# Attention probabilities turned in 32x32 blocks by VectorE and carried across partitions by GpSimd and ScalarE, in place of TensorE transposes, for 12 of 18 jobs

## The chip, the cores and the metric

The kernel runs on one core of a Trainium2 chip. The metric is device time in microseconds: 2020.84 us, median of 3 runs (2015.42 to 2021.22). TensorE (PE) multiplies matrices and writes to PSUM, VectorE (DVE), ScalarE (ACT) and GpSimd (POOL) work elementwise, and the SP, ACT and POOL queues issue DMAs.

## The reference, cut to what matters

A decoder layer for a prompt of 2048 tokens and 8 sequences of 8 sample tokens. One input projection feeds three groups; their outputs (width 2048) go through one output projection. The change lies in the third group, attention of 4 heads of 128 into 256 memory tokens:

```
qx = q_x.reshape(B, T, XA_HEADS, XA_HEAD_DIM)
s = jnp.einsum('bthd,bshd->bhts', qx, mem_k).astype(jnp.float32) * (XA_HEAD_DIM ** -0.5)
p = jax.nn.softmax(s, axis=-1).astype(x.dtype)
y_xa = jnp.einsum('bhts,bshd->bthd', p, mem_v).reshape(B, T, XA_WIDTH) * jax.nn.silu(z_x)
...
y = jnp.concatenate([y_ml, y_cv, y_xa], axis=-1) @ w_out
```

The scores come out with tokens on partitions, and the product with the values needs the 256 memory tokens there: every 128x128 piece of the probabilities must be transposed.

## The kernel before

Three stages follow each other: `project` (to about 1346 us), `attend` (to about 1606 us) and `recur`. The engines' programs are written out by hand, each engine runs its own in order, and they wait on counting semaphores. The change is in `attend`.

`attend` runs a loop over 16 tiles of 128 prompt tokens (t = 0 to 15) and a last one, t = 16, for the samples. I number loops by t. Its work comes as 18 jobs: 16 prompt tiles and two sample jobs, which stand ahead of the prompt tiles 7 and 11. Loop t handles the jobs that `due(t)` gives, normally the one of tile t + 1. In a normal loop TensorE does:

- `out_conv(t)`: 24 matmuls of the output projection over the convolution's half. Every fp32 product is made of three (high by high, high by low, low by high). The first waits until `add(t - 1)` has added the previous tile out of the same PSUM bank.
- `turn_p(n)`: 8 transposes of the probabilities (4 heads, 2 halves of 128 memory tokens) into two PSUM banks.
- `scores(n + 1)`: 4 matmuls for the next job.
- `out_xa(t)`: 24 matmuls over the attention's half.
- `weigh_values(n)`: 16 matmuls of the values by `pT`, the turned probabilities.

VectorE does `gate` (the product with the gate path out of PSUM), `xa_low` (low half of the gated tile), `wm_low` (two weight halves, loops 11 to 14), `turn_keys` (one block transpose of 128x1024 of the sample keys, loops 2 to 9), `conv_low`, `largest` (maxima), `normalise`, and `add` of the tile. ScalarE does `xa_high`, `wm_high`, `load_keys` (it issues four DMAs for one sample sequence's keys, loops 0 to 7), `conv_high`, `p_back` (two copies from PSUM to `pT`) and `exps` (four exponentials). GpSimd issues one value load for each of the first eight loops. SP loads tiles and weights and stores the sums in a scratch tensor.

The sample keys are loaded in 32x32 blocks into the tile `ksq`, which lies in the buffer `raw` and has four slots, and VectorE's transpose turns every block where it stands. At t = 14 SP loads the q and k of the first two tiles of `recur` into the same buffer.

## Time and profile before

| | |
|---|---|
| median of 3 runs | 2020.84 us |
| the profiled execution, its time | 2021.7 us |
| its span | 2019.8 us |
| TensorE busy | 2008.2 us, 99% |
| VectorE, ScalarE, GpSimd busy | 1474.5, 912.9, 874.6 us |
| granted TensorE clock, mean | 0.999 of full speed |

The span is what the profile covers, the time of the execution lies 1.9 us above it. All times in rows are from the start of the span. An engine's idle time costs only where TensorE comes to wait for it.

### The profile page before, as it was taken

To read this page: it belongs to the slowest core of one execution; us is meant where nothing else is said; L and a number is where in the kernel's file an instruction comes from. 1 tells how busy PE (TensorE), PEld (TensorE's weight loads), DVE (VectorE), ACT (ScalarE), POOL (GpSimd) and SP (SyncE) were. 2 spreads that over 40 slices of the span, in tenths; PEclk is the share of its full clock that TensorE was granted. 3 is DMA by queue.
4 is the path that set the end of the run, shared out by engine and by line. 5 is a ranking of instruction groups with operands and counts; after the bars stand their busy time and mean duration, and the time that the engine had idled before them with its cause. 6 is when DMAs were issued, how large, how long until landed. Compare 5 with 4: busy or idle time off the path is not lost.

```text
span 2019.8 us, 34158 instructions
## 1 busy us (share of the span) xinstructions
PE 2008.2 (99%) x12151; PEld 1877.8 (93%) x12151; DVE 1474.5 (73%) x2336; ACT 912.9 (45%) x1863; POOL 874.6 (43%) x721
## 2 busy tenths in 40 slices
PE   9999999999999999999999999999999999999998
PEld 6999999999999999999999999998888888888886
DVE  7777787798778877897778767654445468777775
ACT  5554445445444455454454455442324333433332
POOL 2556555585555565575555555520000122222220
PEclk9999999999999999999999999999999999999999
DMA  6655667555646676555445566578746788888765
GB/s 205 155 142 142 150 152 162 128 141 124 152 122 152 158 171 134 137 143 122 120 131 138 126 157 144 134 212 188 172 115 183 201 250 261 272 239 237 235 180 121
DMA packets 600151, 333.69 MB, mean 165 GB/s; under 512 B 331296, under 2 KB 563888, under 8 KB 599984
## 3 DMA queue, kind: packets, MB, share of 16 engines
q1 hardware_dynamic: 561824, 312.90, 59.5%
q10 hardware_dynamic: 37008, 14.43, 2.9%
q0 software_dynamic: 1152, 4.19, 0.6%
q8 instruction: 98, 1.61, 0.4%
q14 instruction: 69, 0.57, 0.1%
HBM read 237.87 MB, written 93.58 MB: 164 GB/s over the span
## 4 chain that ended last, share of the span: by engine, by line
PE 93%; DVE 2%; SPq 2%; DMA 1%; issue 1%; ACT 0%; POOL 0%; DVEq 0%; POOLq 0%; ACTq 0%
PE bank L742 21%; PE bank L744 21%; PE bank L743 21%; PE bank L2294 3%; PE bank L2296 2%; PE bank L2295 2%; PE bank L2264 2%; PE bank L2249 2%; PE bank L1650 1%; PE bank L1651 1%; PE bank L1652 1%; PE bank L1636 1%; PE bank L1639 1%; PE bank L1637 1%; PE bank L1601 1%; PE bank L1566 1%
## 5 line engine op out<-in xcount | busy, mean ns | idle before, releaser
L742 PE MATMUL bank<-xh,wh 128*128 128x352 f32 x2688 | 869.3, 323 | 0.9 <-DVE stage L1111 0.9
L744 PE MATMUL bank<-xh,wl 128*128 128x352 f32 x2688 | 867.0, 323 | 0.0
L743 PE MATMUL bank<-xl,wh 128*128 128x352 f32 x2688 | 863.6, 321 | 0.0
L1093 DVE TENSOR_TENSOR wl<-raw,wh 128x512 fp32r<-128x512 f32 x384 | 407.4, 1063 | 166.5 <-ACT wh L881 165.5
L742 PEld LDWEIGHTS bank<-xh,wh 128*128 128x128 f32 x2688 | 504.6, 188 | 3.8 <-issue 2.0
L743 PEld LDWEIGHTS bank<-xl,wh 128*128 128x128 f32 x2688 | 507.4, 189 | 0.3 <-issue 0.2
L744 PEld LDWEIGHTS bank<-xh,wl 128*128 128x128 f32 x2688 | 506.3, 188 | 0.0
L903 ACT ACTIVATE snap<-bank 128x352 f32<-128x352 f32 x384 | 178.5, 465 | 374.3 <-PE bank L744 374.2
L881 ACT ACTIVATE wh<-raw 128x512 fp32r<-128x512 f32 x384 | 240.6, 628 | 156.8 <-PE bank L744 155.6
L1093 DVE TENSOR_TENSOR wl<-wt,wh 128x512 fp32r<-128x512 f32 x288 | 246.8, 860 | 85.1 <-ACT wh L881 84.2
L692 POOL TENSOR_TENSOR stage<-snap 128x352 f32<-128x352 f32 x96 | 100.8, 1050 | 440.7 <-ACT snap L903 428.1
L881 ACT ACTIVATE wh<-wt 128x512 fp32r<-128x512 f32 x288 | 180.2, 626 | 118.9 <-PE bank L744 112.7
L676 POOL TENSOR_TENSOR wt<-raw 128x512 f32<-128x512 f32 x96 | 153.6, 1600 | 56.0 <-DMA raw<-in_w_in 42.1
L683 POOL TENSOR_TENSOR wt<-raw,wt 128x512 f32<-128x512 f32 x96 | 154.8, 1613 | 49.8 <-DVE wl L1093 49.8
L1111 DVE TENSOR_TENSOR stage<-bank,snap 128x352 f32<-128x352 f32 x288 | 149.0, 517 | 34.8 <-PE bank L744 30.6
L2143 POOL TENSOR_TENSOR work<-area,mask 128x512 f32<-128x512 f32 x16 | 20.7, 1295 | 336.8 <-DMA area<-scr_a 211.2
L679 POOL TENSOR_TENSOR wt<-raw,wt 128x512 f32<-128x512 f32 x96 | 156.0, 1625 | 8.1 <-DVE wl L1093 0.7
L680 POOL TENSOR_TENSOR raw<-raw 128x512 f32<-128x512 f32 x96 | 158.7, 1653 | 0.0
L2294 PE MATMUL bank<-wm_h,out_yh 128*128 128x512 f32 x240 | 117.1, 488 | 0.0
L2296 PE MATMUL bank<-wm_h,out_yl 128*128 128x512 f32 x240 | 94.3, 393 | 0.0
L2295 PE MATMUL bank<-wm_l,out_yh 128*128 128x512 f32 x240 | 94.0, 392 | 0.0
L2725 DVE SCALAR_TENSOR_TENSOR m_wide<-m_wide,wcb,bank 128x257 f32<-128x257 f32 x120 | 56.9, 475 | 49.6 <-PE bank L2264 48.4
(346 smaller groups left out, 2599.0 us busy)
## 6 DMA issues: line engine op xcount, KB each, us to landing
raw<-in_w_in SPq DMA_DIRECT2D x72, 1024.0 KB, 5.8
raw<-in_w_in SPq DMA_DIRECT2D x48, 512.0 KB, 5.6
scr_vob<-stage SPq DMA_DIRECT2D x192, 88.0 KB, 3.6
scr_qk<-stage SPq DMA_DIRECT2D x48, 352.0 KB, 5.2
raw<-scr_qk SPq DMA_DIRECT2D x16, 1024.0 KB, 8.8
area<-scr_vob SPq DMA_DIRECT2D x32, 512.0 KB, 8.0
scr_acc<-x_res SPq DMA_DIRECT2D x17, 512.0 KB, 6.2
m_acc<-scr_acc SPq DMA_DIRECT2D x17, 512.0 KB, 7.6
```

The source lines that it names most:

```text
L676: pool.tensor_tensor(wt[:, 0], b12, b11, ALU.subtract).then_inc(S["t_ready"], 1)
L679: pool.tensor_tensor(wt[:, 1], b22, wt[:, 0], ALU.subtract).then_inc(S["t_ready"], 1)
L680: pool.tensor_tensor(b12, b22, b12, ALU.subtract).then_inc(S["t_ready"], 1)
L683: pool.tensor_tensor(wt[:, 2], b21, wt[:, 1], ALU.subtract).then_inc(S["t_ready"], 1)
L742: pe.matmul(out, wh[:, b, k, :], xh[:, b, k, :], start=(first and k == 0), stop=False, skip_group_check=True)
L743: pe.matmul(out, wh[:, b, k, :], xl[:, b, k, :], start=False, stop=False, skip_group_check=True)
L744: m = pe.matmul(out, wl[:, b, k, :], xh[:, b, k, :], start=False, stop=(k == 3), skip_group_check=True)
L881: act.activation(halves(q, b)[0], source(q, b), ACT.Copy).then_inc(S["w_high"], 1)
L903: act.activation(snap[:, n, :], g if n == 1 else b, ACT.Copy).then_inc(S["snap"], 1)
L1093: dve.tensor_tensor(low, source(q, b), high.bitcast(F32), ALU.subtract).then_inc(S["w_low"], 1)
L1111: dve.tensor_tensor(out, src, snap[:, add, :], ALU.add).then_inc(S["out_dve"], 1)
L2294: pe.matmul(out, h[:, k, :], wmh[:, k, c], start=(k == 0), stop=False)
```

## The change

Jobs 0 and 1, the two sample jobs and the job right behind each keep the way over TensorE (`by_pe`, 6 jobs). The other 12 (`by_block`, handled in loops 1 to 5, 7 to 9 and 11 to 14) go as follows. VectorE turns every 32x32 block of the probabilities within itself with one transpose of 128x1024 into slot 3 of `ksq` (`turn_blocks`), behind `xa_low`. A block (g, f) of every 128x128 piece must then move from partition group g to group f. That takes 16 copies, each of 32 partitions by 8 runs of 32 elements, for all heads and halves at once: ten by GpSimd (`move_blocks`) and six by ScalarE (`p_moves`), the latter behind `load_keys` and ahead of `conv_high`. TensorE's `weigh_values` waits for all 16. `turn_p` and `p_back` are left out for these jobs. The keys keep three slots. SP's load of `q` and `k` for `recur` is split: the first half still at t = 14, the second at t = 15, behind the last copy. GpSimd's value loads move from a row of their own into the loop. In `project` two semaphores are merged with others, and in `recur` two waits name new counts.

```diff
+    psq = ksq[:, 3, :].rearrange("p (h s t) -> p h s t", h=H, s=2)
...
         jobs.append(("t", t))
     at = {job: n for n, job in enumerate(jobs)}
     s_at = [at["s", 0], at["s", 1]]
+
+    by_pe = [n for n, (kind, t) in enumerate(jobs) if n < 2 or "s" in (kind, jobs[n - 1][0])]
+    by_block = [n for n in range(len(jobs)) if n not in by_pe]
+    POOL_MOVES = [(g, f) for g in range(4) for f in range(4)][:10]
+    ACT_MOVES = [(g, f) for g in range(4) for f in range(4)][10:]
+
+    def turned_by_pe(n):
+        return sum(x < n for x in by_pe)
+
+    def turned_in_blocks(n):
+        return sum(x < n for x in by_block)
+
+    def p_block(tile, part, column):
+        return tile[SQ * part:SQ * (part + 1), :, :, SQ * column:SQ * (column + 1)]
 
     def due(t):
 
...
                 load_x(t + 1)
             if t == WM_FIRST + KM // 2:
                 sp.wait_ge(S["s_KT_ready"], DB)
-                for a in range(2):
-                    sp.dma_start(qk_tiles(raw)[:, a, :, :],
-                                 w["qk"][:, :, a * P:(a + 1) * P].rearrange("f p t -> p f t")).then_inc(S["qk_loaded"], 16)
+            if t >= NT - 2:
+                a = t - (NT - 2)
+                if a:
+                    sp.wait_ge(S["p_moved"], 16 * len(by_block))
+                sp.dma_start(qk_tiles(raw)[:, a, :, :],
+                             w["qk"][:, :, a * P:(a + 1) * P].rearrange("f p t -> p f t")).then_inc(S["qk_loaded"], 16)
 
     @block.gpsimd
     def _(pool):
...
         pool.affine_select(out=smask[:, :], in_=smask[:, :], compare_op=ALU.is_ge, fill=MASKED, base=0,
                            pattern=[[-32, 4], [0, DT]], channel_multiplier=1).then_inc(S["mask_ready"], 1)
         pool.wait_ge(S["mask_ready"], 3)
-        for b in range(DB):
+        def load_values(b):
+            if b >= DB:
+                return
             if b == 0:
                 pool.wait_ge(S["wx_low"], 4)
             else:
                 pool.wait_ge(S["xa_split"], b)
             pool.dma_start(V[:, b, :, :], mem_v[0, b].rearrange("(a s) h d -> s a (h d)", s=P)).then_inc(S[f"s_V_loaded{b // 4}"], 16)
+
+        def move_blocks(n):
+            if n in by_pe:
+                return
+            pool.wait_ge(S["p_squared"], turned_in_blocks(n) + 1)
+            wait(pool, S["pv_summed"], sum(k == "t" for k, _ in jobs[:n]))
+            wait(pool, S["s_pv_summed"], sum(k == "s" for k, _ in jobs[:n]))
+            for g, f in POOL_MOVES:
+                pool.tensor_copy(p_block(pT, f, g), p_block(psq, g, f)).then_inc(S["p_moved"], 1)
+
+        for t in range(NT):
+            load_values(t)
+            for n in due(t):
+                move_blocks(n)
 
     @block.tensor
     def _(pe):
...
                     m.then_inc(S["scores_summed"], 1)
 
         def turn_p(n):
+            if n in by_block:
+                return
             pe.wait_ge(S["p_ready"], 4 * n + 4)
-            wait(pe, S["pT_ready"], 2 * n)
+            wait(pe, S["pT_ready"], 2 * turned_by_pe(n))
             for g in range(4):
                 for s in range(2):
                     m = pe.transpose(bank[TURN[g // 2]][:, (g % 2) * NM + s * P:(g % 2) * NM + (s + 1) * P],
...
         def weigh_values(n):
 
             kind, t = jobs[n]
-            pe.wait_ge(S["pT_ready"], 2 * n + 2)
+            if n in by_pe:
+                pe.wait_ge(S["pT_ready"], 2 * turned_by_pe(n) + 2)
+            else:
+                pe.wait_ge(S["p_moved"], 16 * (turned_in_blocks(n) + 1))
             wait(pe, S["xa_gated"], sum(k == "t" for k, _ in jobs[:n]))
             wait(pe, S["s_pv_copied"], sum(k == "s" for k, _ in jobs[:n]))
             if kind == "t":
...
             if n >= len(jobs):
                 return
             act.wait_ge(S["nb_ready"], n + 1)
-            wait(act, S["p_turned"], 2 * n)
+            wait(act, S["p_turned"], 2 * turned_by_pe(n))
+            wait(act, S["p_squared"], turned_in_blocks(n))
             for g in range(4):
                 act.activation(pr[:, g, :], bank[SCORE[g // 2]][:, (g % 2) * NM:(g % 2 + 1) * NM], ACT.Exp,
                                bias=nb[:, g:g + 1], scale=XA_SCALE, accum_out=sums[:, g:g + 1]).then_inc(S["exp_ready"], 1)
+
+        def p_moves(n):
+            wait(act, S["pv_summed"], sum(k == "t" for k, _ in jobs[:n]))
+            wait(act, S["s_pv_summed"], sum(k == "s" for k, _ in jobs[:n]))
+            act.wait_ge(S["p_squared"], turned_in_blocks(n) + 1)
+            for g, f in ACT_MOVES:
+                act.activation(p_block(pT, f, g), p_block(psq, g, f), ACT.Copy).then_inc(S["p_moved"], 1)
 
         def p_back(n):
             wait(act, S["pv_summed"], sum(k == "t" for k, _ in jobs[:n]))
             wait(act, S["s_pv_summed"], sum(k == "s" for k, _ in jobs[:n]))
             for i in range(2):
-                act.wait_ge(S["p_turned"], 2 * n + i + 1)
+                act.wait_ge(S["p_turned"], 2 * turned_by_pe(n) + i + 1)
                 act.activation(pT[:, 2 * i:2 * i + 2, :, :],
                                bank[TURN[i]].ap().rearrange("p (h s t) -> p h s t", h=2, s=2), ACT.Copy).then_inc(S["pT_ready"], 1)
 
...
             if b >= DB:
                 return
             act.wait_ge(S["wx_low"], 4)
-            wait(act, S["s_KT_ready"], b - 3)
+            wait(act, S["s_KT_ready"], b - 2)
             for j in range(4):
-                act.dma_start(ksq[SQ * j:SQ * (j + 1), b % 4, :].rearrange("p (h i c) -> p h i c", h=H, c=SQ),
+                act.dma_start(ksq[SQ * j:SQ * (j + 1), b % 3, :].rearrange("p (h i c) -> p h i c", h=H, c=SQ),
                               mem_k[0, b, :, :, SQ * j:SQ * (j + 1)].rearrange("(i r) h c -> r h i c", r=SQ)
-                              ).then_inc(S[f"s_K_loaded{b % 4}"], 16)
+                              ).then_inc(S[f"s_K_loaded{b % 3}"], 16)
 
         def wm_high(k):
             if 0 <= k < KM:
...
                 wm_high(2 * (t - WM_FIRST - 1) + n)
             if t:
                 load_keys(t)
-            conv_high(t + 1)
             todo = due(t)
             for n in todo:
-                p_back(n)
+                if n in by_block:
+                    p_moves(n)
+            conv_high(t + 1)
+            for n in todo:
+                if n in by_pe:
+                    p_back(n)
                 if n == todo[-1]:
                     exps(n + 1)
                 else:
...
 
             if not 0 <= b < DB:
                 return
-            dve.wait_ge(S[f"s_K_loaded{b % 4}"], 64 * (b // 4 + 1))
-            dve.transpose(KT[:, b, :, :].rearrange("p h s -> p (h s)"), ksq[:, b % 4, :]).then_inc(S["s_KT_ready"], 1)
+            dve.wait_ge(S[f"s_K_loaded{b % 3}"], 64 * (b // 3 + 1))
+            dve.transpose(KT[:, b, :, :].rearrange("p h s -> p (h s)"), ksq[:, b % 3, :]).then_inc(S["s_KT_ready"], 1)
 
         def xa_low(t):
             dve.wait_ge(S["xa_high"], t + 1)
...
             ch.sync()
             for g in range(4):
                 dve.tensor_scalar(pr[:, g, :], pr[:, g, :], rsum[:, g:g + 1], None, ALU.mult).then_inc(S["p_ready"], 1)
+
+        def turn_blocks(n):
+            dve.wait_ge(S["p_ready"], 4 * n + 4)
+            wait(dve, S["p_moved"], 16 * turned_in_blocks(n))
+            dve.transpose(ksq[:, 3, :], area[:, 0:1024]).then_inc(S["p_squared"], 1)
 
         def gate(t):
             dve.wait_ge(S[f"xz_loaded{t % 2}"], 16 * (t // 2 + 1))
...
             else:
                 dve.wait_ge(S["cleared"], 1)
             xa_low(t)
+            for n in due(t):
+                if n in by_block:
+                    turn_blocks(n)
             for n in range(2):
                 wm_low(2 * (t - WM_FIRST - 1) + n)
             turn_keys(t - 2)
...
         pool.wait_ge(S["res_added"], 2)
         pool.wait_ge(S["wm_high"], 1)
         pool.wait_ge(S["acc_stored0"], 16)
-        for b in range(4):
-            pool.wait_ge(S[f"s_K_loaded{b}"], 64 * 2)
+        for b in range(3):
+            pool.wait_ge(S[f"s_K_loaded{b}"], 64 * (3 - b // 2))
         for a in range(2):
             pool.wait_ge(S[f"s_V_loaded{a}"], 16 * 4)
         cleared = S["cleared"]
```

On TensorE, in loop 2, the rows between `out_conv` (L1639, after the change L1678) and `out_xa` (L1650, L1689) are, before:

```order
L1639 MATMUL bank<-convw,out_yl 128x512
L1587 MATMUL bank<-ident,area 128x128 [waits pT_ready_attend,p_ready_attend]
L1587 MATMUL bank<-ident,area 128x128 x7
L1566 MATMUL bank<-work,area 128x256 [waits xq_loaded1_attend,exp_ready_attend]
L1566 MATMUL bank<-work,area 128x256 x3
L1650 MATMUL bank<-x_wx_h,out_yh 128x512 [waits xa_split_attend]
L1651 MATMUL bank<-x_wx_l,out_yh 128x512
```

and with the change:

```order
L1678 MATMUL bank<-convw,out_yl 128x512
L1600 MATMUL bank<-work,area 128x256 [waits xq_loaded1_attend,exp_ready_attend]
L1600 MATMUL bank<-work,area 128x256 x3
L1689 MATMUL bank<-x_wx_h,out_yh 128x512 [waits xa_split_attend]
L1690 MATMUL bank<-x_wx_l,out_yh 128x512
```

The transposes L1587 are gone and nothing stands in their place; `scores` follows the convolution at once.

On ScalarE, in loop 3, from `xa_high` (L1706, L1745) to `exps` (L1714, L1754), before:

```order
L1706 ACTIVATE out_yh<-area 128x512 [waits out_summed_attend,xa_gated_attend]
L1732 DMA raw<-in_cache_mem_k 32x32x32 [waits s_KT_ready_attend,wx_low_attend]
L1732 DMA raw<-in_cache_mem_k 32x32x32 x3
L1698 ACTIVATE out_yh<-area 128x512 [waits cv_used_attend,yc_loaded1_attend]
L1722 ACTIVATE area<-bank 128x512 [waits p_turned_attend,pv_summed_attend]
L1722 ACTIVATE area<-bank 128x512 [waits p_turned_attend]
L1714 ACTIVATE area,work<-bank,work 128x256 [waits p_turned_attend,nb_ready_attend]
L1714 ACTIVATE area,work<-bank,work 128x256 x3
```

and with the change:

```order
L1745 ACTIVATE out_yh<-area 128x512 [waits out_summed_attend,xa_gated_attend]
L1779 DMA raw<-in_cache_mem_k 32x32x32 [waits s_KT_ready_attend,wx_low_attend]
L1779 DMA raw<-in_cache_mem_k 32x32x32 x3
L1762 ACTIVATE area<-raw 32x8x32 [waits p_squared_attend,pv_summed_attend]
L1762 ACTIVATE area<-raw 32x8x32 x5
L1737 ACTIVATE out_yh<-work 128x512 [waits cv_used_attend,yc_loaded0_attend]
L1754 ACTIVATE area,work<-bank,work 128x256 [waits p_squared_attend,p_turned_attend,nb_ready_attend]
L1754 ACTIVATE area,work<-bank,work 128x256 x3
```

The six copies L1762 stand between the issue of the keys (L1732, L1779) and `conv_high` (L1698, L1737), and the two `p_back` copies L1722 are gone.

On SP's queue, from the store of tile 13 to the first gate loads of `recur` (L1401, L1402), before:

```order
L1502 DMA scr_acc<-x_res 128x1024 [waits res_added_attend]
L1498 DMA x_res<-in_x_prompt 128x1024 [waits acc_stored1_attend]
L1531 DMA raw<-scr_qk 128x16x128 [waits s_KT_ready_attend]
L1531 DMA raw<-scr_qk 128x16x128
L1502 DMA scr_acc<-x_res 128x1024 [waits res_added_attend]
L1498 DMA x_res<-in_x_sample 64x1024 [waits acc_stored0_attend]
L2020 UNCONDITIONAL_BRANCH
L1401 DMA area<-scr_negr 128x4x128 [waits cv_split_attend,xa_gated_attend,cleared_attend]
L1402 DMA area<-scr_a 128x4x128
```

and with the change:

```order
L1517 DMA scr_acc<-x_res 128x1024 [waits res_added_attend]
L1513 DMA x_res<-in_x_prompt 128x1024 [waits acc_stored1_attend]
L1549 DMA raw<-scr_qk 128x16x128 [waits s_KT_ready_attend]
L1517 DMA scr_acc<-x_res 128x1024 [waits res_added_attend]
L1513 DMA x_res<-in_x_sample 64x1024 [waits acc_stored0_attend]
L1549 DMA raw<-scr_qk 128x16x128 [waits p_moved_attend]
L2079 UNCONDITIONAL_BRANCH
L1401 DMA area<-scr_negr 128x4x128 [waits cv_split_attend,xa_gated_attend,cleared_attend]
L1402 DMA area<-scr_a 128x4x128
```

The second `raw<-scr_qk` has moved past a store and a load, to right ahead of the gate loads of `recur`.

## Rows read from the trace of the kernel before

**Rows 1.** The page, busy time of each engine, its share of the span and instructions
```profile
PE 2008.2 (99%) x12151; PEld 1877.8 (93%) x12151; DVE 1474.5 (73%) x2336; ACT 912.9 (45%) x1863; POOL 874.6 (43%) x721
```

**Rows 2.** Busy time in loops 3 and 7: length, then each engine
```profile
1396.77:1412.06 15.29, 15.29 (x81) 13.15 (x81) 7.39 (x14) 4.16 (x12) 0.72 (x1) 1.00 0.79 190
1463.40:1478.77 15.37, 15.37 (x82) 13.15 (x81) 8.33 (x19) 5.29 (x18) 0.00 (x0) 1.00 0.71 163
```

**Rows 3.** The chain that ended last, 1372 to 1560 us: start, us, what
```profile
1417.52 0.87 PE bank L1587 x8
...
1425.58 1.78 PE bank L1601 x16
...
1543.70 1.78 PE bank L1601 x16
```

**Rows 4.** Timeline of ScalarE, loops 2 and 3: start, us, instruction, idle before
```profile
1382.29 4.90 ACTq L1732 DMA_DIRECT2D raw<-in_cache_mem_k  x4
...
1397.59 4.62 ACTq L1732 DMA_DIRECT2D raw<-in_cache_mem_k  x4
1402.32 0.64 ACT L1698 ACTIVATE out_yh<-work 128x512 fp32r<-128x512 f32 x1 [4.11 <-PE bank L1639]
```

**Rows 5.** Timeline of VectorE, loop 3
```profile
1398.24 0.69 DVE L1811 TENSOR_TENSOR out_yl<-area,out_yh 128x512 fp32r<-128x512 f32 x1 [0.70 <-ACT out_yh L1706]
1398.85 1.24 DVE L1806 STREAM_TRANSPOSE s_kv<-raw 128x1024 f32<-128x1024 f32 x1
1402.99 0.69 DVE L1798 TENSOR_TENSOR out_yl<-work,out_yh 128x512 fp32r<-128x512 f32 x1 [2.89 <-ACT out_yh L1698]
```

**Rows 6.** Timeline of ScalarE, then VectorE, loop 7
```profile
1466.60 4.53 ACTq L1732 DMA_DIRECT2D raw<-in_cache_mem_k  x4
1471.23 0.63 ACT L1698 ACTIVATE out_yh<-work 128x512 fp32r<-128x512 f32 x1 [4.06 <-issue]
...
1477.26 1.28 DVE L1853 TENSOR_TENSOR x_res<-x_res,bank 128x512 f32<-128x512 f32 x2
```

**Rows 7.** Timeline: an add that TensorE waits for, and the matmuls behind
```profile
1412.13 0.40 PE L1637 MATMUL bank<-convw,out_yh 128*128 128x512 f32 x1
...
1600.59 0.69 DVE L1853 TENSOR_TENSOR x_res<-x_res,bank 128x512 f32<-128x512 f32 x1 [1.96 <-PE bank L1652]
...
1601.67 0.39 PE L1637 MATMUL bank<-convw,out_yh 128*128 128x512 f32 x1
```

**Rows 8.** Groups of ScalarE's instructions, 1345 to 1606 us
```profile
L1692 ACT ACTIVATE x_wx_h<-raw 128x1024 fp32r<-128x1024 f32 x4 | 4.0, 1056 | 2.0 <-PE bank L744 2.0
...
L1698 ACT ACTIVATE out_yh<-work 128x256 fp32r<-128x256 f32 x1 | 0.4, 418 | 4.1 <-PE bank L1639 4.1
```

**Rows 9.** Timeline of ScalarE, start of the stage
```profile
1345.79 2.97 ACT L1692 ACTIVATE x_wx_h<-raw 128x1024 fp32r<-128x1024 f32 x3 [1.96 <-PE bank L744]
```

**Rows 10.** Groups of GpSimd's instructions, whole span
```profile
L676 POOL TENSOR_TENSOR wt<-raw 128x512 f32<-128x512 f32 x96 | 153.6, 1600 | 56.0 <-DMA raw<-in_w_in 42.1 <-DVE wl L1093 13.8
...
L2147 POOL TENSOR_TENSOR m_wide<-raw,area 128x256 f32<-128x256 f32 x60 | 49.2, 830 | 16.3 <-PE bank L2250 16.3
...
L2165 POOL TENSOR_SCALAR m_few<-m_few 128x4 f32<-128x4 f32 x16 | 3.1, 193 | 66.1 <-ACT area L2474 41.8 <-ACT m_wide L2474 24.2
```

**Rows 11.** One line of VectorE in the first stage: ns min/median/max
```profile
L1093 DVE TENSOR_TENSOR wl<-raw,wh x384: 647/1012/3711, 36.7 to 1329.1; 128x512 fp32r<-128x512 f32 x192
```

**Rows 12.** Timeline of SP's queue, end of the stage
```profile
1578.67 3.06 SPq L1531 DMA_DIRECT2D raw<-scr_qk  x2
...
1596.76 1.64 SPq L1413 DMA_DIRECT2D area<-scr_z  x1
1601.31 3.60 SPq L2077 DMA_DIRECT2D scr_acc<-x_res  x1
```

**Rows 13.** Timeline of VectorE, loop 11
```profile
1542.71 0.68 DVE L1853 TENSOR_TENSOR x_res<-x_res,bank 128x512 f32<-128x512 f32 x1
```

More of the change, by code:

```diff
@@ L658, in _ @@
         pool.memset(eps[:, :], EPS).then_inc(S["eps_ready"], 1)
-        pool.memset(ident[:, :], 0.0).then_inc(S["ident_zero"], 1)
-        pool.wait_ge(S["ident_zero"], 1)
+        pool.memset(ident[:, :], 0.0).then_inc(S["ident_ready"], 1)
+        pool.wait_ge(S["ident_ready"], 1)
         pool.affine_select(out=ident[:, :], in_=ident[:, :], compare_op=ALU.not_equal, fill=1.0, base=0,
@@ L787, in turn_states @@
             pe.transpose(bank[7][0:72, 0:P], cnew.ap().rearrange("p s w j -> p (s w j)"), ident[:, :]).then_inc(S["states_turned"], 1)
-        pe.wait_ge(S["ident_ready"], 1)
+        pe.wait_ge(S["ident_ready"], 2)
         for k in range(WARM):
@@ L1324, in _ @@
         dve.wait_ge(S["gains_turned"], 1)
-        dve.tensor_copy(gcol[:, :], bank[7][:, 0:2 * KD]).then_inc(S["gains_ready"], 1)
-        dve.wait_ge(S["gains_ready"], 1)
+        ch.step(dve.tensor_copy(gcol[:, :], bank[7][:, 0:2 * KD]))
+        ch.sync()
         for u in range(2):
@@ L2208, in turn_keys @@
                 pe.wait_ge(before["exp_ready"], 4 * (NT + 2))
-                pe.wait_ge(before["pT_ready"], 2 * (NT + 2))
+                pe.wait_ge(before["pT_ready"], 2 * 6)
             wait(pe, S["t1_ready"], 4 * t)
```

## The prediction

> **What bounds the kernel now.** I read the page's busy times first: TensorE is busy 2008.2 of a span of 2019.8 us [rows 1]. So the only things worth looking for are work taken from TensorE and waits put in front of it. The change touches the middle stage (memory attention and the first half of the output projection, 1346 to 1606 us), so next I read busy time per loop: loop 3, from one end of the value matmuls to the next, is 15.29 us long and TensorE is busy in all of it, VectorE in 7.39, ScalarE in 4.16; loop 7 is 15.37 long and just as full, but VectorE and ScalarE have 8.33 and 5.29 [rows 2]. The chain that ended last runs along TensorE there: a loop holds one group of 8 transposes of 0.87 us and ends with the 16 value matmuls of 1.78 us [rows 3]. The timelines of ScalarE and VectorE then tell how far behind TensorE their chain runs [rows 4, 5, 6], and that decides this case.
>
> **Part 1, the transposes go: the gain.** In 12 loops TensorE no longer issues the 8 transposes. With no wait in their place a loop takes 15.30 - 0.87 = 14.43 us, and 12 x 0.87 = 10.4 us leave the path [rows 3]. The two ScalarE copies out of PSUM go too; they lay behind the wait for the maxima and freed nothing.
>
> **Part 2, VectorE turns blocks.** One transpose of 128x1024 stands behind the low half of the gated tile. The same operation on keys takes 1.24 us [rows 5]. In loop 3 the low half ends at 1398.93; the new transpose would end near 1400.2 and the key transpose near 1401.4, before VectorE's next input (the convolution's low half, 1402.99) is there. So it is covered by the idle time before 1402.99, in key loops and in the plain ones. In loops 11 to 14 two 128x1024 subtractions fill that time instead. In loop 11 the first add starts at 1542.71; pushed back by 1.24 and with 0.68 for itself it ends at 1544.63. TensorE goes on 0.39 after an add (1601.28 to 1601.67) [rows 7], at 1545.02. Unstalled, its second convolution matmul follows the end of the value matmuls by 0.07 (1412.06 to 1412.13), here 1543.70 + 1.78 + 0.07 - 0.87 = 1544.68 [rows 3, 7, 13]. Loss 0.3 us; uncovered fully it would be 1.24.
>
> **Part 3, six ScalarE copies ahead of the convolution's high half.** No copy of 32x8x32 is in the trace. The nearest is a 128x256 copy of 418 ns [rows 8]; three 128x1024 copies of 1056 ns took 2.97 us in a row, so (2.97 - 1.06) / 2 = 0.96 from start to start, 0.10 less than one lasts [rows 8, 9]. Lower value 0.32 each, 1.92 for six. Upper, if a change of partition group empties the engine, 0.42 each, 2.5 for six. I take 0.32, since all copies in this stage overlap so. What stands ahead of them in loops 1 to 5 and 7 is the issue of four key DMAs, which keeps the queue 4.62 to 4.90 us [rows 4]. In loop 3 it ends at 1402.21 and the high half starts at 1402.32; nothing is free there, and the whole 1.92 moves the high half. Behind it on the path: low half, maxima, exponentials, normalising, then the add of the output tile, for which TensorE's next convolution waits. Loop 7 shows this chain without a pause: high half at 1471.23, first add from 1477.26 for half of 1.28, so 6.7 us [rows 6].
> Loop 2: 1382.29 + 4.90 + 0.05 + 1.92 + 6.7 + 0.39 = 1396.25, against 1396.77 + 0.07 - 0.87 = 1395.97 unstalled: 0.3 us lost. Loop 3: 1397.59 + 4.62 + 9.06 = 1411.27 against 1411.26: nothing. VectorE's second add also ends some 0.2 us after the next gate could have begun, which makes the next loop late. I take 0.25 for each of loops 1 to 5, 1.3 us.
> Loop 7 comes after a sample job and begins late: its issue ends at 1466.60 + 4.53 = 1471.13, plus 9.06 is 1480.19, against 1478.77 + 0.07 - 0.87 = 1477.97. Loss 2.2 us [rows 2, 6].
> Loops 8 and 9 issue no keys: ScalarE waits there for TensorE anyway and the six copies are covered. In loops 12 to 14 they follow the weight halves and end about when the convolution releases the high half. With no cover each block would cost up to 1.9 to 2.5.
>
> **Part 4, ten GpSimd copies.** GpSimd had nothing but one value load a loop. They start when the blocks are turned (about 3.5 us into a loop) and must end by 14.43 - 1.78 = 12.65, when the value matmuls are due. Bounds: 0.19 us, the cost of a 4 element operation, and 0.83, a 128x256 product with two inputs; in the first stage 128x512 takes 1.60, half of which is 0.80 [rows 10]. One input and 256 elements lie between; I take 0.5, so ten end at 8.5, covered by 4 us.
> They share something with VectorE, though: the same subtraction of 128x512 takes 647 ns at best and 1012 as a median in the first stage, beside a busy GpSimd [rows 11], and 0.69 here [rows 5]. The convolution's low half now runs at about 8.4 us, under the last copies, and in loop 11 the two subtractions do. I put 0.15 on each of five key loops after the first (with loop 7) and 0.2 on loop 11: 1.0 us, bounds 0 and 0.4 on each of eleven.
> The Trainium skill (SBUF — State Buffer, Who interferes with whom) has a stricter rule: a VectorE instruction with two SBUF inputs and a GpSimd instruction that reads SBUF exclude each other for a whole instruction. By that rule a low half waits for at most one copy, so by it, with the 0.5 that I took, the sum would lose up to 0.5 a loop where I have 0.15, some 2 us more; no run yet shows how many hit.
>
> **Part 5, the queues.** The keys now have three slots; the wait asks for a transpose of the loop before, long done. The two halves of the first q and k tiles (two 1 MB DMAs, 3.06 us of issue at 1578.67) part: the second goes behind the last store of the stage and ahead of the next stage's gates. SP's queue is busy from there to 1596.76 + 1.64 = 1598.40 and idle until 1601.31, so 1.5 us more of issue fit into 2.9 [rows 12]. The next one took 3.60 us to issue, a sign of full rings, so I put 0.7 us on this place, bounds 0 and 4. What is behind it are the gates and value loads of the next stage's first tiles. Moving the count of a semaphore to another name, in the first stage, costs nothing.
>
> **Sum.** -10.4 + 0.3 (loop 11) + 1.3 + 2.2 (key loops) + 1.0 + 0.7 = -4.9 us. The profiled execution took 2021.7 us, 0.9 above the median of the runs, and would take 2016.8; against the median of 2020.84 this is **2015.9 us**.
>
> **Rivals.**
> All of it hidden. If the issue of keys ends earlier once the loops are arranged anew, or the high half's chain shortens by the 2 us that I charge, the loops are TensorE's at 14.43: 2020.84 - 10.4 = 2010.4. For it: six of the twelve loops issue no keys at all. Against: in loop 3 0.1 us was free. Chance 0.15.
> ScalarE's copies do not overlap. Then 0.6 more in loops 2 to 5, 7 and 11, 3.6 us, and with a low half that hits a GpSimd copy each time about 1 more: 2020.4, no change. Against: copies of this stage overlap. Chance 0.17.
> GpSimd's copies are late, the one on the slower side. Its place is the wait of the value matmuls. It decides from (12.65 - 3.5) / 10 = 0.91 us a copy on, and outweighs the 0.87 at 1.0. At 1.1 the matmuls wait for 3.5 + 11 - 12.65 = 1.9 us in each of the 12 loops, 1.0 more than is saved: 2020.84 + 12 = 2032.8. For it: strided runs of 32 elements between partition groups, of which no row speaks, and neighbours of 0.80 and 0.83. Against: these read twice. Chance 0.14.
> The forecast itself: 0.52; its own range is 2012.5 to 2018.
> Something else: 0.02.
>
> **Numbers.** 0.3% is 6.1 us, about what a measurement here can tell from none. A third of the forecast's case lies below 2014.8, and all of the hidden one: faster 0.34. The rest of the forecast, most of the non-overlapping case and the near end of late copies: same 0.50. Slower 0.16. From the hidden case's edge, 2010.5, to 2022, past the non-overlapping one, about 2 in 10 is left out, most of it late copies; I go to 2023.
>
> **What would show it.** Transposes: TensorE's 8 short matmuls gone from 12 loops, and loops 8, 9, 12, 13 at 14.4 us. Key loops at 14.5 to 14.9, with idle TensorE before the convolution, released by the add. Loop 7 near 16.6. ScalarE's copies 0.32 apart, GpSimd's 0.5. The prediction is wrong if TensorE waits before the value matmuls (copies late), if the copies are over 0.4 apart, if no wait shows at the add in loop 7, or if TensorE idles for more than 3 us between 1600 and 1670 more than before.

## Result: 0.17% slower, and the profile after

| | before | after |
|---|---|---|
| median, 22 runs each | 2021.59 us | 2024.99 us |
| ratio | | 1.0017 [1.0010, 1.0025] |
| span of the profiled execution | 2019.8 us | 2023.1 us |
| loops 1 to 14, first to last convolution | 223.62 us | 225.83 us |

The forecast was 2015.9 us, faster by 4.9. The kernel became slower by 3.4 us (2.0 to 5.1 by the interval), above the end of the stated range, 2023, and on the other side of the old time; the rival in which ScalarE's copies do not overlap (2020.4) came nearest. Single executions of these kernels now and then take far longer (one of the 22 after took 2469 us, one in experiment 2 took 4029), and the ratios leave them out.

The page of the changed kernel, against [rows 1]: the 96 transposes are gone from TensorE and took 7.9 us of busy time with them, yet the span grew by 3.3. So TensorE now idles where it did not.

```profile
PE 2000.3 (99%) x12055; PEld 1868.0 (92%) x12055; DVE 1483.8 (73%) x2348; ACT 931.4 (46%) x1911; POOL 931.8 (46%) x841
```

The view of waits names the place (TensorE, 1350 to 1606 us; columns: what waits, for what, us in total, times, the longest):

```profile
PE bank L1675 <- DVE x_res L1909: 10.1, 7, 2.9
```

9.8 of it, six of the seven waits, is the first convolution matmul of a loop, L1675, that waits for the add of the tile before, L1909. The seventh, 0.33 us at 1604.09, stands behind loop 15, and the kernel before has the same one (0.33 at 1601.34). The value matmuls, L1640, do not appear. By stretches, against [rows 2], with the loop starts of this trace (loops 1, 2, 3, 4, 7, 8 and 12; columns as in [rows 2]):

```profile
1366.34:1383.19 16.85, 14.75 (x75) 12.42 (x73) 6.59 (x14) 5.79 (x17) 4.61 (x11) 1.00 0.82 189
1383.19:1399.19 16.00, 16.00 (x72) 13.47 (x73) 8.59 (x16) 5.68 (x16) 4.62 (x11) 0.89 0.85 197
1399.19:1415.73 16.54, 14.67 (x76) 12.40 (x74) 7.79 (x15) 5.68 (x16) 4.60 (x11) 1.00 0.71 176
1415.73:1431.99 16.26, 14.67 (x72) 12.38 (x73) 8.14 (x16) 5.69 (x16) 4.62 (x11) 1.00 0.72 179
1467.62:1485.24 17.62, 14.70 (x75) 12.39 (x74) 9.01 (x20) 7.04 (x22) 3.93 (x10) 1.00 0.60 145
1485.24:1499.65 14.41, 14.41 (x72) 12.30 (x73) 8.66 (x16) 5.68 (x16) 4.29 (x10) 1.00 0.41 129
1550.67:1565.07 14.40, 14.40 (x72) 12.30 (x73) 10.21 (x17) 7.77 (x18) 6.15 (x10) 1.00 0.66 199
```

Loops 8 and 12 got what the change promises: 14.4 us, TensorE full. Loops 1, 3, 4 and 7 are longer than before (15.42, 15.30, 15.30, 15.37), and in each TensorE is idle for 1.6 to 2.9 us. Loop 2 is different: TensorE is busy in all of it, but at a mean granted clock of 0.89.

The timeline of loop 3, ScalarE first, then VectorE and TensorE, against [rows 4, 5, 7], shows the chain that ends at the add:

```profile
1400.32 5.82 ACTq L1779 DMA_DIRECT2D raw<-in_cache_mem_k  x4
1406.24 2.61 ACT L1762 ACTIVATE area<-raw 32x256 f32<-32x256 f32 x6 [5.35 <-issue]
1408.87 0.63 ACT L1737 ACTIVATE out_yh<-work 128x512 fp32r<-128x512 f32 x1
...
1401.53 1.24 DVE L1887 STREAM_TRANSPOSE raw<-area 128x1024 f32<-128x1024 f32 x1
...
1409.54 0.69 DVE L1849 TENSOR_TENSOR out_yl<-work,out_yh 128x512 fp32r<-128x512 f32 x1 [5.64 <-ACT out_yh L1737]
1414.90 1.28 DVE L1909 TENSOR_TENSOR x_res<-x_res,bank 128x512 f32<-128x512 f32 x2
...
1415.73 0.47 PE L1675 MATMUL bank<-convw,out_yh 128*128 128x512 f32 x1 [1.87 <-DVE x_res L1909]
```

Read it from the end: TensorE waited 1.87 us for an add that began 6.03 us after the high half (1408.87 to 1414.90); the high half stood behind six copies of 2.61 us, and those behind 5.82 us of DMA issue. From the keys' first issue to the high half it was 1402.32 - 1397.59 = 4.73 us before [rows 4] and is 8.55 now: 1.2 from a longer issue, 2.6 from the copies.

Loop 7, where the forecast saw the largest loss, has the same chain with the issue as short as before (4.53 in [rows 6]):

```profile
1471.06 4.56 ACTq L1779 DMA_DIRECT2D raw<-in_cache_mem_k  x4
1475.75 2.61 ACT L1762 ACTIVATE area<-raw 32x256 f32<-32x256 f32 x6 [4.12 <-issue]
1478.38 0.63 ACT L1737 ACTIVATE out_yh<-work 128x512 fp32r<-128x512 f32 x1
...
1484.41 1.28 DVE L1909 TENSOR_TENSOR x_res<-x_res,bank 128x512 f32<-128x512 f32 x2
```

The two kinds of block copies as groups (1366 to 1604 us; busy us and mean ns of one, then idle time before):

```profile
L1762 ACT ACTIVATE area<-raw 32x256 f32<-32x256 f32 x72 | 29.8, 414 | 34.3 <-issue 24.7 <-DVE raw L1887 4.0 <-DVE s_kv L1857 4.0
L1583 POOL COPY area<-raw 32x256 f32<-32x256 f32 x120 | 56.8, 473 | 160.8 <-DVE raw L1887 154.5
```

And the start of loop 2 on TensorE, behind the first wait:

```profile
1383.19 0.47 PE L1675 MATMUL bank<-convw,out_yh 128*128 128x512 f32 x1 [2.10 <-DVE x_res L1909]
...
1384.18 0.46 PE L1676 MATMUL bank<-convw,out_yh 128*128 128x512 f32 x1
1384.43 0.63 PE L1678 MATMUL bank<-convw,out_yl 128*128 128x512 f32 x1
1384.86 0.63 PE L1675 MATMUL bank<-convw,out_yh 128*128 128x512 f32 x1
...
1387.42 0.56 PE L1675 MATMUL bank<-convw,out_yh 128*128 128x512 f32 x1
1387.82 0.39 PE L1676 MATMUL bank<-convw,out_yh 128*128 128x512 f32 x1
```

One microsecond after the wait the matmuls go from 0.23 to 0.43 us apart, and back after 3.4 us. The granted clock of the stretch around it is 0.53 and of the rest of the loop 1.00, so the clock was at its lower level, 1.2 GHz, for nearly all of that stretch:

```profile
1384.20:1387.80 3.60, 3.60 (x10) 2.84 (x9) 2.90 (x4) 0.63 (x1) 0.83 (x3) 0.53 0.74 154
1387.80:1399.19 11.39, 11.39 (x60) 9.79 (x59) 4.68 (x12) 5.05 (x15) 3.78 (x9) 1.00 0.96 228
```

**Where the time went.** "Loss" is a loop's length after, less what it would have been if only the 0.88 us of the transposes had gone (its length before less 0.88).

| loops | forecast | measured loss | of it |
|---|---|---|---|
| 1, 3, 4, 5 | 0.25 each, 1.0 | 2.31, 2.12, 1.84, 0.44 = 6.7 | waits 2.10, 1.87, 1.60, 0.18 |
| 2 | 0.25 | 1.58 | lower clock, no wait |
| 7 | 2.2 | 3.13 | wait 2.92 |
| 11 | 0.3 | 1.36 | wait 1.12 |
| contention, spread | 1.0 | 0.26, within loop 11 (experiment 7) | |
| 8, 9, 12 to 14 and 6 | 0 | 0.0 | |
| all | 4.8 | 12.8 | |

Twelve transposes gone give 12 x 0.88 = 10.6, so the loops end 2.2 us worse. The remaining 1.1 us of the span's 3.3 lie outside them: 0.5 before loop 1 and 0.6 behind loop 14. Beside each wait stand another 0.2 us or so, about as much as two matmuls overlap elsewhere: one lasts 0.39 and the next starts 0.23 after it.

### The profile page after: what moved, and what is told of

Read it like the earlier page. It is cut to its first block, busy times and chain, and to the rows that moved or that the text cites. A ratio compares the mean times of both kernels' runs of the same rounds, so it can differ in the third digit from the quotient of the medians.

```text
span 2023.1 us, 34157 instructions
## 1 busy us (share of the span) xinstructions
PE 2000.3 (99%) x12055; PEld 1868.0 (92%) x12055; DVE 1483.8 (73%) x2348; ACT 931.4 (46%) x1911; POOL 931.8 (46%) x841
## 4 chain that ended last, share of the span: by engine, by line
PE 89%; DVE 3%; SPq 2%; DMA 2%; ACT 1%; issue 1%; ACTq 1%; POOL 0%; DVEq 0%; POOLq 0%
PE bank L742 21%; PE bank L744 21%; PE bank L743 21%; PE bank L2353 3%; PE bank L2355 2%; PE bank L2354 2%; PE bank L2323 2%; PE bank L2308 2%; PE bank L2284 1%; PE bank L2309 1%; PE bank L1675 1%; PE bank L1689 1%; PE bank L1678 1%; PE bank L1676 1%; PE bank L1690 1%
## 5 line engine op out<-in xcount | busy, mean ns | idle before, releaser
L1583 POOL COPY area<-raw 32x256 f32<-32x256 f32 x120 | 56.8, 473 | 160.8 <-DVE raw L1887 154.5
```

## Experiments

Ratios are to the kernel before on the same chip; "loops" is the length of loops 1 to 14 in the profiled execution (223.62 before, 225.83 changed). It is the finer measure, since the rest of the span varies by several us from one execution to the next. A wait "in" a loop is the one at its end.

**1. The same copies, behind the high half instead of ahead of it.**

```diff
             todo = due(t)
+            conv_high(t + 1)
             for n in todo:
                 if n in by_block:
                     p_moves(n)
-            conv_high(t + 1)
```

> The changed kernel with one swap on ScalarE: the convolution's high half first, the six copies behind it, ahead of the exponentials. Theory (the copies stand on the chain key issue, high half, maxima, exponentials, normalising, add, for which TensorE waits): the 2.6 us leave that chain, since the exponentials wait for the maxima anyway; the waits of TensorE at the add (10.1 us in 7 loops) shrink to under 1.5 us, nearly all 12 loops come to 14.4 to 14.6 us, and the time to 2021.6 - 10.4 + 1 = 2012, 2010.5 to 2014. Rival 1 (the longer issue of keys, or GpSimd's copies beside VectorE, cost the time wherever ScalarE's copies stand): key loops stay over 15 us, time above 2019. Rival 2 (the fallen TensorE clock behind a wait costs most): with the waits gone the clock stays at 1.0, which reads like the theory, but then loops without a fall (3, 4, 7) should already have been short.

Measured: 2012.17 us, 0.9957 [0.9940, 0.9973], loops 214.89. The waits at the add shrink from 10.1 to (0.33 of it again behind loop 15):

```profile
PE bank L1675 <- DVE x_res L1909: 1.4, 3, 0.8
```

Same instructions, same engines, one place in a row: 0.6% by the ratios, 12 us, of which 10.9 in these loops. Three loops still lose: loop 1 0.34, loop 7 1.02, loop 11 0.44. With the issue of the keys where it is, the copies' place was the fault, not their cost.

**2. All 16 copies on GpSimd.** `POOL_MOVES` takes 16 blocks, `ACT_MOVES` none.

> All 16 copies on GpSimd, none on ScalarE. GpSimd's copies took 0.445 us each in key loops and 0.61 in the loops with weight halves. Theory: ScalarE's chain is as before the change, so key loops come to 14.5; 16 copies end at 3.5 + 7.1 = 10.6 us in a loop, ahead of 12.65. In loops 11 to 14 they take 9.8 and start about 4.7, so the value matmuls wait for GpSimd some 1 to 2 us there and 3 in loop 14. Sum 2021.6 - 10.4 + 6 = 2017, 2013 to 2020. Rival (contention of GpSimd and VectorE is what costs): more of it, key loops above 15.5, time above 2025.

Measured: 2019.67 us, 0.9993 [0.9983, 1.0004]. The kernel was run once more for its trace.

> The kernel in which GpSimd carries all 16 blocks and ScalarE none, run once more for its trace. ScalarE's 2.6 us ahead of the high half are gone, so the waits at the add of loops 1, 2, 3 and 7 (2.10, 1.87, 1.60, 2.92 us) should be under 0.5, and the clock should not fall in loop 2. GpSimd needs 16 x 0.445 = 7.1 us in a key loop, done by 10.7 of 14.4, and 16 x 0.62 = 9.9 in the weight loops 11 to 14, done at 13.4 or later where the matmuls are due at 12.65: a wait of 0.8 to 2 us before the value matmuls there, 4 to 6 in all. Rival: the waits at the add stay over 1 us, since the issue of keys alone is what is late.

Measured in that run: 2017.61 us, loops 220.97. TensorE's waits have changed place:

```profile
PE bank L1640 <- POOL area L1583: 5.8, 5, 2.6
PE bank L1675 <- DVE x_res L1909: 0.6, 2, 0.3
```

Loops 1 to 4 are 14.50, 14.42, 14.42 and 14.92, loop 7 is 15.35; loops 11 to 14 are 17.34, 15.02, 15.03 and 15.20. (The four waits that the expectation lists stand in loops 1, 3, 4 and 7.) With ScalarE's copies gone the keys' issue alone is nearly hidden (at 6.52 us in loop 4 a wait of 0.26 is left), and GpSimd is late in loop 7 (0.62) and where VectorE's weight halves run beside it (2.62, 0.30, 0.32 and 1.92 in loops 11 to 14): the rival "GpSimd's copies are late" is real, at 16 copies, not at ten. Behind the 1.92 us the clock fell, and loop 15 took 12.30 us against 10.98:

```profile
1583.43 2.46 PE L1640 MATMUL bank<-area 128*128 128x128 f32 x16 [1.92 <-POOL area L1583]
...
1585.50:1589.50 4.00, 4.00 (x14) 3.20 (x14) 1.38 (x2) 0.63 (x1) 0.00 (x0) 0.65 0.82 188
```

**3. The transposes put back as idle work.** In the 12 block loops TensorE also transposes the identity eight times; nothing reads the result.

> The changed kernel, and TensorE does 8 transposes of the identity into the same banks in each of the 12 block loops, results unused (0.87 us of TensorE work a loop). Theory (the key loops run at the length of the ScalarE and VectorE chain): loops 1 to 4 and 7 stay as long as in the changed kernel, the waits at the add shrink by 0.87; loops 8, 9, 12, 13, 14 grow by 0.88 and loops 5 and 11 by 0.7 and 0; sum +5, 2030. Rival (TensorE sets the length everywhere, the waits are a side effect): +10.4, 2035.4.

Measured: 2028.55 us, 1.0041 [1.0029, 1.0053], loops 229.92. The waits fall to 0.48, 0.32, 2.01 and 0.25 in loops 1, 4, 7 and 11, and that of loop 3 is gone. Loops 12 and 13 are at 15.33 and loop 14 at 13.61, against 15.30 and 13.58 before: loops without a wait grow by the full length of the transposes. Loops 7 and 11, whose waits were longer than that, keep their length to 0.01 (17.62 and 15.84) while the wait shrinks by 0.91 and 0.87. In loops 1, 3 and 4 the keys' issue was also shorter in this execution (5.89, 4.70 and 5.17 us, against 6.53, 5.82 and 5.52), so they show it less cleanly. The end of a loop is set by whichever of the two chains is later. Loop 8 took 16.94, since the clock fell behind the 2.01 us.

**4. Another order of ScalarE's blocks**, (2,2), (3,2), (3,3), (2,3), (3,0), (3,1), so that some neighbours change only the source group, some only the target group, and one pair both.

> The six copies of ScalarE in another order, so that two of the five steps keep the target partition group and change the source group, one keeps the source and changes the target, and the last two keep the source. Read in the trace is the time from start to start. If a change of the target group empties ScalarE's pipe: 0.43 at those steps and 0.32 at the two that keep the target. If a change of either does: 0.43 at all. Time as the changed kernel, less at most 6 x 0.2 = 1 us.

Measured: 2029.02 us in one run, loops 227.26; six copies still take 2.60 to 2.61 us, so every step is 0.43 to 0.44. (The fourth step, from (2,3) to (3,0), changes both groups, which the expectation overlooks; it changes nothing in the reading.) Its waits in loops 1 and 7 (3.00 and 3.17) are like those of experiments 6 and 7, so the one time says little; the spacing is the result.

**5. Blocks only in the five loops that have no keys and follow no sample job.**

```diff
-    by_pe = [n for n, (kind, t) in enumerate(jobs) if n < 2 or "s" in (kind, jobs[n - 1][0])]
+    by_pe = [n for n in range(len(jobs)) if n not in (10, 11, 15, 16, 17)]
```

> Only five loops that issue no keys and follow no sample job (8, 9, 12, 13, 14) go by blocks; the other 13 jobs keep TensorE's transposes. If the new order itself is sound and only the key loops and those behind a sample job spoil it, five loops shrink from 15.3 to 14.4 us and nothing else moves: 2021.6 - 5 x 0.88 + 0.5 for the split load at the stage's end = 2017.7 us, 2017.0 to 2018.5, a ratio of 0.998. If the loss in the changed kernel comes from something spread over all loops (a clock that falls, contention, the split load), nothing is gained here either: 2020.5 to 2022.

Measured: 2016.78 us, 0.9984 [0.9974, 0.9994], loops 219.20: 4.42 less than before, 0.88 in each of the five. The loss is local to the loops with keys and the two behind sample jobs.

**6. ScalarE's copies within one partition group** (`p_block(psq, f, g)` as source, order (3,3), (2,3), (2,2), (3,2), (3,1), (3,0)).

> ScalarE's six copies read and write the same partition group (the blocks then are not carried, which leaves that part of the computation out): two in group 3, two in group 2, one in group 1, one in group 0. If a crossing between groups hinders overlap, all six are 0.32 us apart, 1.95 us in all, and the waits at the add of loops 1, 2, 3 and 7 shrink by 0.65. If a change of group between neighbours hinders it, the first two and the third and fourth are 0.32 apart and the others 0.43. If copies of 32 partitions or of runs of 32 elements never overlap, all stay 0.43 apart, six in 2.60, and the time stays at 2025.

Measured: 2025.78 us in one run, loops 225.57. The six copies of loop 3:

```profile
1405.62 2.34 ACT L1762 ACTIVATE area<-raw 32x256 f32<-32x256 f32 x6 [4.12 <-issue]
```

2.34 is what two steps of 0.32, three of 0.43 and one copy of 0.41 give: a copy starts before the last one's end only where both keep the group. In the changed kernel no two neighbours can, since each of the 16 copies has its own pair of source and target group. The waits are 3.25, 0.24, 0.94 and 2.62 in loops 1, 3, 4 and 7. That of loop 1 grew and did not shrink, since the keys' issue took 7.80 us there; in loop 7 it shrank by 0.30, for copies that are 0.27 shorter.

**7. Without GpSimd's ten copies.**

> The changed kernel without GpSimd's ten copies (ten of 16 blocks are then not carried, which leaves that part of the computation out); ScalarE's six stay. Theory: GpSimd's copies are hidden and cost only contention, VectorE's weight halves 1.42 against 1.28 us and low halves 0.70 against 0.69, and the waits at the add stay within 0.3 us of 2.10, 1.87, 1.60 and 2.92: 2024, 2023 to 2025. Rival: GpSimd's copies are what makes the issue of keys longer in loops 3 and 4 (5.8 and 5.5 us); then it falls back to 4.6 to 4.9 and about 2 us come back: 2022 or less.

Measured: 2022.52 us, 1.0015 [1.0006, 1.0025], loops 227.10; ratios of this and the changed kernel overlap. The keys' issue is no shorter without GpSimd (7.47, 5.13, 4.74, 5.26 in loops 1 to 4), so GpSimd does not cause it. The waits follow it: 3.56, 0.79 and 1.31 in loops 1, 3 and 4, where the expectation had them unchanged, and 2.86 in loop 7. VectorE's slower weight half is back at 1.28 us from 1.42, and one loop is shorter without GpSimd: loop 11, 15.59 against 15.85. There a small operation of VectorE ahead of the exponentials had run beside the copies, first with them, then without:

```profile
1546.16 0.41 DVE L1873 TENSOR_SCALAR work<-work 128x4 f32<-128x4 f32 x1
...
1547.38 0.17 DVE L1872 TENSOR_SCALAR work<-work 128x4 f32<-128x4 f32 x1
```

**8. The keys issued behind the exponentials; copies left where the change put them.**

```diff
-            if t:
-                load_keys(t)
             todo = due(t)
...
+            load_keys(t)
             if t == 0:
-                load_keys(0)
```

> The changed kernel with one thing moved: the four key DMAs are issued behind the exponentials, not ahead of the six copies. If issue plus copies ahead of the high half are what makes TensorE wait at the add, the waits of loops 1 to 5 and 7 shrink to under 0.5 us. The issue (4.6 to 5.8 us) now begins where ScalarE has 4.3 us free before the next gated tile, so it may be 0.3 to 1.5 us late for that and give some back: 2013, 2011.5 to 2016. Rival: the copies alone, at 2.6 us ahead of the high half, are too much, with or without keys: 2019 or more.

Measured: 2013.64 us, 0.9965 [0.9950, 0.9980], loops 215.42. Loops 2 to 4 are 14.42; waits of 0.86 and 1.12 remain in loops 7 and 11. In loop 3 ScalarE now has (its exponentials left out):

```profile
1395.79 2.61 ACT L1762 ACTIVATE area<-raw 32x256 f32<-32x256 f32 x6 [1.97 <-DVE raw L1885]
1398.42 0.63 ACT L1737 ACTIVATE out_yh<-work 128x512 fp32r<-128x512 f32 x1
...
1401.39 0.60 ACTq L1779 DMA_DIRECT2D raw<-in_cache_mem_k  x1
1402.02 0.70 ACTq L1779 DMA_DIRECT2D raw<-in_cache_mem_k  x1
1402.74 3.32 ACTq L1779 DMA_DIRECT2D raw<-in_cache_mem_k  x1
1406.10 0.70 ACTq L1779 DMA_DIRECT2D raw<-in_cache_mem_k  x1
1407.60 0.63 ACT L1745 ACTIVATE out_yh<-area 128x512 fp32r<-128x512 f32 x1 [4.37 <-DVE area L1891]
```

The copies are the same 2.61 and sit ahead of the high half as in the changed kernel, and no wait follows. In loops 1 to 5 neither the issue nor the copies were too long; their sum was. In loops 7 and 11, behind the sample jobs, the copies alone are still too much. The four issues take 5.41 us here, three of 0.6 to 0.7 us and one that stands for 3.3, and behind the exponentials that costs nothing. Loop 11 issues no keys, so its wait of 1.12 is what it was.

**9. The kernel before, with the keys issued behind the exponentials.**

> The kernel before with only the issue of keys moved behind the exponentials. If nothing of the chain behind ScalarE holds TensorE there, it does nothing: loops 1 to 5 stay at 15.3 to 15.4, 2021.6, ratio 1.000. Rival: part of what the moved issue gives in the changed kernel is a gain that has nothing to do with the blocks (less contention, shorter issue): 0.1 us or more in each of six loops, 2020 or less.

Measured: 2022.14 us, 1.0006 [0.9994, 1.0018], loops 223.61. The move is worth nothing without the blocks, so what experiment 8 gained, it gained by taking the issue off the chain that the copies had made late.

**10. The kernel before, with the q and k load split as in the change.**

> The kernel before with one part of the change alone: the second half of the q and k load issued one loop later, behind the store and the load of that loop. The sum had 0.7 us for it with bounds 0 and 4. Stage ends and the rest of the changed kernel differ by 0.5 us from before, so 2022.1 against 2021.6, a ratio within 1.0005. Rival: the split is a gain or a loss of its own of more than 1 us, which the changed kernel's trace hides under its other waits.

Measured: 2022.07 us, 1.0010 [0.9998, 1.0022], loops 223.62. From the start of loop 15 to the end of the span it takes 430.11 us, against 430.38 before; the changed kernel takes 430.93. The trace shows no cost; the interval leaves up to 4.4 us open. In this execution the keys' issue of loop 1 took 6.14 us, with the order of before, and loop 1 stayed at 15.42. (In experiment 5, which has that order in loop 1 too, it took 6.57, and the loop 15.41.)

**11. Both moves: keys behind the exponentials, copies behind the high half.**

> Both moves at once: ScalarE's six copies behind the high half, the issue of keys behind the exponentials. Ahead of the high half then stands only the high half of the gated tile. If the rest of the loss in the two single moves (waits of 0.86 and 1.12 us in loops 7 and 11 with the keys moved, 0.82 and 0.21 and 0.4 in loop 1 with the copies moved) is what still stands ahead of the high half, all of it goes and 12 loops run at 14.42 to 14.9: 2011, 2009.5 to 2013, a wait of under 0.3 us at any add. Rival: the issue, now 2.6 us later than with the keys moved alone, is late for the next gated tile and the key loops lose 0.5 to 1.5 us each: 2014 to 2018.

Measured: 2011.87 us, 0.9959 [0.9944, 0.9974], loops 213.45, 10.2 less than before. Waits of TensorE (0.33 of the 0.5 behind loop 15, as before) and busy time of loops 2, 7 and 12:

```profile
PE bank L1675 <- DVE x_res L1907: 0.5, 2, 0.3
```

```profile
1379.78:1394.20 14.42, 14.42 (x76) 12.31 (x74) 8.39 (x15) 5.68 (x16) 4.96 (x11) 1.00 0.81 208
1458.21:1472.66 14.45, 14.45 (x75) 12.31 (x74) 9.80 (x20) 7.03 (x22) 4.29 (x10) 1.00 0.90 205
1537.19:1551.63 14.44, 14.44 (x72) 12.30 (x73) 10.40 (x17) 7.76 (x18) 6.15 (x10) 1.00 0.69 205
```

Only loop 11 still loses (0.45, of it a wait of 0.21). Experiments 1, 8 and this one are faster than both kernels; the times do not tell them apart. The loops do: 214.89, 215.42 and 213.45.

## Why the prediction was wrong

**Part 1, right.** 0.88 us leave each loop that has no wait; in experiment 11 that is nearly the whole story.

**Part 2, right in size, wrong in loop 11.** VectorE's transposes take 1.24 us and are covered in the plain loops. In loop 11 the forecast charged 0.3 for VectorE alone. Measured are 1.36, and with the copies behind the high half (experiment 1) 14.93 - 14.49 = 0.44: the other 0.9 come of the place of ScalarE's copies, for which the forecast had charged nothing in this loop.

**Part 3, the failing step.** The place was right: the copies move the high half one for one, and from there to the start of the add it is 6.03 us, as in [rows 6]. Two sizes were wrong. "I take 0.32, since all copies in this stage overlap so" fell: they are 0.44 apart, six take 2.61 (experiments 4 and 6 show the condition). That is 0.7 us in each of seven loops, 4.9 us, the forecast's whole gain (that the two numbers agree is chance); the rival that priced this had 0.42 and the same seven loops less one. By the forecast's own list of signs, "over 0.4 apart" is the one that came true. And the keys' issue was carried over as 4.62 to 4.90 from one execution. In the changed one it is 6.53 (1367.08 to 1373.61), 4.75, 5.82, 5.52 and 4.44 in loops 1 to 5, and experiments 10 and 5 have 6.14 and 6.57 in loop 1 with the old order: the 4.66 of before is the short one of ten (5.9 us or more in loop 1 of every other execution that issues the keys in this place). In the loops of before that spread can't be seen, since slack lay behind it; [rows 4] show two of its values. The two corrections added to the forecast come within about 0.5 us of the measured loss in each of these loops:

| loop | forecast + copies + issue | measured |
|---|---|---|
| 1 | 0.25 + 0.7 + 1.87 = 2.8 | 2.31 |
| 3 | 0.25 + 0.7 + 1.20 = 2.15 | 2.12 |
| 4 | 0.25 + 0.7 + 0.77 = 1.7 | 1.84 |
| 5 | 0.25 + 0.7 - 0.39 = 0.6 | 0.44 |
| 7 | 2.2 + 0.7 + 0.03 = 2.9 | 3.13 |

Loop 2 by the same sum is 0.25 + 0.7 - 0.15 = 0.8, against 1.58, and loop 11, which issues no keys, is the case of part 2.

**Not foreseen: the clock.** A wait of TensorE was priced as its own length. Behind the 2.10 us in loop 1 the clock dropped, and TensorE took 1.6 us longer for the work of loop 2. That stands in place of the 0.8 or so that loop 2 would have waited. In experiment 4 the clock stayed up, and loop 2 waited 0.96 us and lost 1.19. So in loop 2 the clock cost some 0.4 to 0.8 us more than a wait would have; that estimate is from these two executions.

**Part 4, right on the main point.** Ten copies take 4.45 us in a key loop (0.445 each, 0.5 assumed), the value matmuls never wait, and in the loops with weight halves they take up to 6.7 and still fit. Of the 1.0 us of contention only 0.26 shows, in loop 11 (experiment 7). The 0.15 on a low half was a fair size where the two meet: 0.76 us in loops 8 and 9, 0.80 to 0.88 in experiment 11, against 0.69. But in loops 8 and 9 it is covered, and in the key loops the low half now comes behind GpSimd's last copy (in loop 3 that ends at 1407.29 and the low half starts at 1409.54). The rule quoted from the Trainium skill (SBUF — State Buffer, Who interferes with whom) would have cost some 0.5 a loop; loops 8 and 12 run at 14.4, so nothing of it reaches TensorE there.

**Part 5, too small to tell.** 0.7 was charged; experiment 10 shows no cost in the trace. The idle time of SP's queue ahead of 1601.31 was used up all the same: the second half took 0.59 us to issue, but the loads behind it took longer, and the issue of the last of them ended 12.22 us behind the start of loop 15, against 8.98 before.

The claim for the hidden case was "if the issue of keys ends earlier once the loops are arranged anew". It does not by itself. When it is arranged so, the loops shorten by 8.2 us (experiment 8) and 10.2 us (experiment 11) of the 10.4 of that case.

## What to carry to other kernels

A loop with one engine at 100% has a second chain right behind it. Before work is put ahead of an instruction, ask what waits for that instruction, not whether the engine has idle time: ScalarE was busy for 4.16 of 15.29 us [rows 2], which does not even count the 4.62 us of its DMA issue [rows 4], and 2.6 us ahead of the high half cost 12 us of the kernel against the same 2.6 us behind it. When work leaves the bound engine the loop shortens, and the slack of every other chain shrinks by the same amount, so durations that had never mattered (a DMA issue of 4.6 or 6.1 us) begin to. And where a term hangs on one duration from one execution with slack behind it, price its spread too.

## What the runs showed of the hardware

- ScalarE copies of 32 partitions x 256 fp32 elements last 0.40 to 0.42 us and start about 0.32 us apart where neighbours keep both partition groups, 0.43 to 0.44 where the source or target group changes. On GpSimd the same copy takes 0.445 us from start to start, and those across groups no more than those within one. Beside VectorE's 128x1024 weight halves two of the ten take 1.36 and 1.28 us (loop 11), and all ten 6.7. VectorE pays too: 1.42 for 1.28 us on a weight half, 0.76 to 0.88 for 0.69 on a low half, 0.41 for 0.17 on an operation of 128x4.
- TensorE's clock, which had been full, fell to 1.2 GHz behind seven of the nine waits at the add that were longer than 2 us (2.10, 2.01, 3.17, 3.25, 2.62, 3.56 and 2.86 us; not behind 2.92 and 3.00), and behind none of the shorter ones there (the longest 1.87). It fell between the last 0.5 us of the wait (2.86) and some 1.2 us after it (3.56), and stayed down for 3 to 3.4 us. The loop behind it took 1.4 to 1.6 us longer than TensorE's work there takes at the full clock, so such a wait can cost nearly twice itself. In experiment 2's second run the clock also fell behind a wait of 1.92 us ahead of the value matmuls (1.3 us longer), and not behind one of 2.62 there. Why some were spared stays open.
- Four key DMAs of 128 KB (32x32x32 elements) keep ScalarE's queue for 4.4 to 7.8 us in loops 1 to 5 where they are issued ahead of the high half (7.80 in loop 1 of experiment 6, 7.47 in that of experiment 7), and for 2.8 to 4.1 us in loop 6, which is 5 us longer. Most of it is one or two of the four. What sets the spread was not found; it is not GpSimd.
